# Rope halves exchanged by ScalarE, shared key tiles, and another order of both mixers in a four-layer transformer kernel

## What is computed

```
# mixer A: u, va, q, k, v, qi, ki, wi, g_a, g_b = split(h @ w_in)
y_a = (gelu(u) * spatial(layer_norm(gelu(va)))) @ w_pa    # spatial: a causal 128x128 token mix in each of 4 groups
q, k, qi, ki = rope(...)                     # 8 heads of 64; halves x1, x2: x1*cos - x2*sin, x2*cos + x1*sin
score = sum_h relu(qi_h . ki) * wi_h         # the top 64 keys of each query are kept
y_b = attention(q, k, v, kept keys) @ w_pb
out = (sigmoid(g_a) * y_a + sigmoid(g_b) * y_b) @ w_out
# mixer B: four branches on h = rmsnorm(x), 4 heads of 64
a: window attention at three dilations      b: latent attention, rope on 32 of 96 columns (kpe shared by the heads)
c: compressed blocks (kc, vc -> gelu MLP) + selected keys (ks, vs) + window keys (kw, vw), gated
d: stick-breaking attention
merged = sum_i sigmoid(h @ w_merge_i + b_i) * ((y_i * silu(gate_i)) @ w_branch_i);   x = x + merged @ w_out
```

## Time and profile before

| | us |
|---|---|
| median of 3 runs | 1652.29 (1651.14 to 1652.61) |
| the profiled execution | 1651.31 |
| its span | 1649.5 |
| PE busy | 1594.4 (97%) |
| DVE, ACT, POOL busy | 504.5, 366.6, 1000.3 |
| mean granted clock of PE | 0.976 |

### The profile page before, as it was taken

One profiled execution on the slowest core, in us unless ns is written; L12 is line 12 of the kernel. 1 busy time (PEld: TensorE's weight loads), 2 busy tenths in 40 slices (PEclk: granted clock), 3 DMA queues, 4 the chain that ended last, 5 costly groups with the idle time before them and its releaser, 6 DMA issues.

```text
span 1649.5 us, 32224 instructions
## 1 busy us (share of the span) xinstructions
PE 1594.4 (97%) x14172; PEld 1396.0 (85%) x14172; DVE 504.5 (31%) x1128; ACT 366.6 (22%) x902; POOL 1000.3 (61%) x542
## 2 busy tenths in 40 slices
PE   7999999999999999999999999979999999999998
PEld 5888788887888888878888888868788887788887
DVE  3111264343110211125534311133433233533323
ACT  2111124212110211111422211023333122324212
POOL 6777555666777577764566677744165664346571
PEclk9999999999999999999999999979989999989999
DMA  9565444554555465544455555534354554434461
GB/s 358 202 205 205 141 173 160 179 205 163 200 203 203 176 214 201 201 167 154 162 176 201 178 201 198 197 104 158 132 175 144 198 179 164 150 127 167 173 205 52
DMA packets 42619, 294.90 MB, mean 179 GB/s; under 512 B 4720, under 2 KB 6256, under 8 KB 7792
## 3 DMA queue, kind: packets, MB, share of 16 engines
q1 hardware_dynamic: 42480, 292.84, 50.9%
HBM read 291.78 MB, written 1.05 MB: 178 GB/s over the span
## 4 chain that ended last, share of the span: by engine, by line
PE 95%; DVE 2%; ACT 1%; issue 1%; POOL 0%; DMA 0%; SPq 0%; DVEq 0%; ACTq 0%
PE ps L510 27%; PE ps L511 27%; PE ps L512 27%; PE ps L528 2%; PE ps L530 1%; PE ps L529 1%; PE ps L760 1%; PE ps L596 1%; PE ps L602 1%; PE ps L614 1%; PE ps L588 1%; PE ps L586 0%; DVE diag L1199 0%; POOL w_low L486 0%; DMA ring<-in_w 0%
## 5 line engine op out<-in xcount | busy, mean ns | idle before, releaser
L486 POOL TENSOR_TENSOR w_low<-ring 128x1024 f16<-128x1024 f32 (+2 forms) x538 | 1000.1, 1883 | 616.6 <-DMA ring<-in_w 616.5
L510 PE MATMUL ps<-hP,ring 128*128 128x256 f16 (+1 forms) x2976 | 820.5, 276 | 14.1 <-DVE hP L1209 11.7
L511 PE MATMUL ps<-hP,ring 128*128 128x256 f16 (+1 forms) x2976 | 819.9, 276 | 0.0
L512 PE MATMUL ps<-hP,w_low 128*128 128x256 f16 (+1 forms) x2976 | 819.3, 275 | 0.0
L510 PEld LDWEIGHTS ps<-hP,ring 128*128 128x128 bf16 (+1 forms) x2976 | 294.7, 99 | 62.3 <-DVE hP L1209 13.8
L511 PEld LDWEIGHTS ps<-hP,ring 128*128 128x128 bf16 (+1 forms) x2976 | 294.7, 99 | 36.9
L512 PEld LDWEIGHTS ps<-hP,w_low 128*128 128x128 f16 (+1 forms) x2976 | 294.9, 99 | 36.6
L511 PE MATMUL ps<-work,ring 128*128 128x256 f16 x1088 | 296.7, 273 | 0.0
L510 PE MATMUL ps<-work,ring 128*128 128x256 f16 x1088 | 296.5, 272 | 0.0
L512 PE MATMUL ps<-work,w_low 128*128 128x256 f16 x1088 | 296.3, 272 | 0.0
L1242 DVE TENSOR_TENSOR ps<-work,ps 128x256 f32<-128x256 f32 x88 | 37.8, 429 | 342.1 <-PE ps L512 312.0
(11 more groups left out here) (199 smaller groups left out, 1142.2 us busy)
## 6 DMA issues: line engine op xcount, KB each, us to landing
...
```

The source lines that it names most:

```text
L486: nc.gpsimd.tensor_tensor(w_low[:, c % SLOTS, a:b], ring[:, c % SLOTS, a:b], w_high[:, c % SLOTS, a:b], ALU.subtract).then_inc(split.by((c ...
L510: nc.tensor.matmul(bank, w_high[:, slot, a:a + m], rhs(k, 0), start=(k == 0), stop=False)
L511: nc.tensor.matmul(bank, w_high[:, slot, a:a + m], rhs(k, 1), start=False, stop=False)
L512: mm = nc.tensor.matmul(bank, w_low[:, slot, a:a + m], rhs(k, 0), start=False, stop=(k == kt - 1))
```

## The change

Four things change.
1. The exchange of rope halves leaves TensorE. ScalarE copies 32 partitions at a time crosswise from the bank's first half to its second (`swap`, four copies a tile in A, two in B and one more for each bq to bring its unrotated rows to SBUF). `rotate` on VectorE does the cosine product, the sine product and the addition in one go after it. So that the two halves lie 32 partitions apart in B, the rope columns of kpe and bq are padded with zeros: these tiles have 128 rows instead of 96. SBUF copies (`raw`) and the exchange matrices are gone.
2. ks and kw share one product tile (kc), and so do kc and vc (cmp): two tiles fewer in each mixer B. ScalarE takes kc in four copies of 64 partitions, VectorE takes cmp in eight additions.
3. In A, u and va are made before ga; the layer norm's statistics run before `normalise(s, 1)`, the root follows the copy of turn 1, `y_parts(1)` stands between the two halves of the norm, and the token mix comes after ga5.
4. In B, almost every tile changes its place: qc, kc and cvg before turn(a), the latent branch's products after scores(s), turn(s) between the two hid tiles. Merges 0 to 4 of branch 0 stand around turn(b); the later ones fill the steps of the compressed and stick-breaking branches up to merge (2, 1). `PAIR_B` gives their banks.

The diff, cut to its core (inside functions the indentation is cut by 16):

```diff
-TILES_A = [(kind, n) for kind, m in (("qi", 4), ("ki", 1), ("wi", 2), ("q", 4), ("k", 4), ("v", 4), ("ga", 8), ("u", 4),
-                                     ("va", 4), ("gb", 8)) for n in range(m)]
-TILES_B = [("aq", 0), ("aq", 1), ("ak", 0), ("ak", 1), ("cq", 0), ("ckv", 0), ("rk", 0), ("av", 0), ("av", 1), ("lat", 0),
-           ("ag", 0), ("ag", 1), ("qc", 0), ("rkv", 0), ("qc", 1), ("bk", 0), ("bk", 1), ("bk", 2), ("bk", 3), ("bv", 0),
-           ("bv", 1), ("bq", 0), ("bq", 1), ("kc", 0), ("bq", 2), ("bq", 3), ("kc", 1), ("cvg", 0), ("cvg", 1), ("cmp", 0),
-           ("cmp", 1), ("cg", 0), ("cg", 1), ("bg", 0), ("bg", 1), ("hid", 0), ("hid", 1), ("dq", 0), ("dq", 1), ("kcmp", 0),
-           ("vcmp", 0), ("dk", 0), ("dk", 1), ("dv", 0), ("dv", 1), ("dg", 0), ("dg", 1)]
+TILES_A = [(kind, n) for kind, m in (("qi", 4), ("ki", 1), ("wi", 2), ("q", 4), ("k", 4), ("v", 4), ("u", 4),
+                                     ("va", 4), ("ga", 8), ("gb", 8)) for n in range(m)]
+TILES_B = [("aq", 0), ("aq", 1), ("ak", 0), ("ak", 1), ("cq", 0), ("ckv", 0), ("rk", 0), ("av", 0), ("lat", 0), ("av", 1),
+           ("qc", 0), ("qc", 1), ("kc", 0), ("cvg", 0), ("cvg", 1), ("rkv", 0), ("ag", 0), ("ag", 1), ("cmp", 0), ("cg", 0),
+           ("cg", 1), ("bk", 0), ("bk", 1), ("bk", 2), ("bk", 3), ("bv", 0), ("bv", 1), ("bq", 0), ("bq", 1), ("bq", 2),
+           ("bq", 3), ("hid", 0), ("hid", 1), ("bg", 0), ("bg", 1), ("dq", 0), ("dq", 1), ("dk", 0), ("dk", 1), ("dv", 0),
+           ("dv", 1), ("kcmp", 0), ("vcmp", 0), ("dg", 0), ("dg", 1)]
...
+PAIR_B = {8 * br + n: 2 * ((n + 1) % 2) if br < 3 else 4 + 2 * (n % 2) for br in range(4) for n in range(8)}
...
-def swap(s, t, m, bank, copied, matrix):
-    pe.wait_ge(*raw_copied.at((s,) + t))
-    pe.wait_ge(*cos_done.at((s,) + t))
-    nc.tensor.matmul(ps[0:m, bank, T:2 * T], matrix, copied[0:m, :], start=True, stop=True
...
     first_tiles(s, [(s, "qi", n) for n in range(4)])
     gemm("ki", 0)
-    turn_pairs("qi", 0), turn_pairs("qi", 1)
     gemm("wi", 0), gemm("wi", 1)
-    turn_pairs("qi", 2), turn_pairs("qi", 3)
-    gemm("q", 0)
-    turn_pairs("ki", 0)
-    gemm("q", 1)
-    turn_pairs("q", 0)
+    gemm("q", 0), gemm("q", 1)
     for p, (kind, n) in enumerate((("q", 2), ("q", 3), ("k", 0), ("k", 1))):
         logits(p)
         gemm(kind, n)
-        turn_pairs(*ROPED_A[6 + p])
-    gemm("k", 2)
-    turn_pairs("k", 1)
-    gemm("k", 3)
-    turn_pairs("k", 2)
-    gemm("v", 0)
-    turn_pairs("k", 3)
-    gemm("v", 1), gemm("v", 2)
+    gemm("k", 2), gemm("k", 3)
+    gemm("v", 0), gemm("v", 1), gemm("v", 2)
     pe.wait_ge(*scored.at((s, 7, 1)))
     pe.wait_ge(*taken(s, ("k", 3)))
     unit(0)
-    gemm("v", 3), gemm("ga", 0), gemm("ga", 1), gemm("ga", 2)
+    gemm("v", 3), gemm("u", 0), gemm("u", 1), gemm("u", 2), gemm("u", 3)
     turn(s, 0)
-    gemm("ga", 3)
+    gemm("va", 0)
     values(0)
-    gemm("ga", 4)
+    gemm("va", 1)
     pe.wait_ge(*y_low.at((s, 0)))
     unit(1)
-    gemm("ga", 5), gemm("ga", 6), gemm("ga", 7), gemm("u", 0)
+    gemm("va", 2), gemm("va", 3), gemm("ga", 0), gemm("ga", 1), gemm("ga", 2)
     turn(s, 1)
-    gemm("u", 1)
+    gemm("ga", 3)
     values(1)
-    gemm("u", 2), gemm("u", 3)
-    gemm("va", 0), gemm("va", 1), gemm("va", 2), gemm("va", 3)
-    gemm("gb", 0), gemm("gb", 1), gemm("gb", 2)
...
                                   gmlp("w_s")[:, g * P:g * P + P], start=True, stop=True)
         mm.then_inc(tokens_mixed.by((s, g)), 1)
-    for n in range(5, 8):
+    gemm("ga", 6), gemm("ga", 7)
...
-    gemm("cq", 0), gemm("ckv", 0), gemm("rk", 0), gemm("av", 0)
-    turn_pairs("rk", 0)
-    gemm("av", 1)
+    gemm("cq", 0), gemm("ckv", 0), gemm("rk", 0), gemm("av", 0), gemm("lat", 0), gemm("av", 1)
     pe.wait_ge(*taken(s, ("ak", 1)))
     scores(s, "a", lambda h: head(a_qkT, 0, h), lambda h: head(a_qkT, 2, h))
-    gemm("lat", 0), gemm("ag", 0), gemm("ag", 1), gemm("qc", 0), gemm("rkv", 0), gemm("qc", 1)
+    gemm("qc", 0), gemm("qc", 1), gemm("kc", 0), gemm("cvg", 0), gemm("cvg", 1), gemm("rkv", 0), gemm("ag", 0)
+    turn(s, "a")
+    gemm("ag", 1)
+    mix(s, "a", lambda t, h: a_v[:, t, h * HD:h * HD + HD])
+    gemm("cmp", 0)
+    pe.wait_ge(*y_low.at((s, "a")))
+    pe.wait_ge(*taken(s, ("kc", 0)))
+    scores(s, "s", lambda h: head(c_qkT, 0, h), lambda h: half(c_qkT[:, 2, :], h))
+    gemm("cg", 0), gemm("cg", 1)
     for n in range(4):
         gemm("bk", n)
     gemm("bv", 0), gemm("bv", 1)
-    turn(s, "a")
-    gemm("bq", 0), gemm("bq", 1), gemm("kc", 0)
-    mix(s, "a", lambda t, h: a_v[:, t, h * HD:h * HD + HD])
-    turn_pairs("bq", 0)
-    gemm("bq", 2)
-    turn_pairs("bq", 1)
-    gemm("bq", 3), gemm("kc", 1)
-    turn_pairs("bq", 2), turn_pairs("bq", 3)
-    pe.wait_ge(*y_low.at((s, "a")))
-    pe.wait_ge(*taken(s, ("kc", 1)))
-    scores(s, "s", lambda h: head(c_qkT, 0, h), lambda h: half(c_qkT[:, 2, :], h))
-    gemm("cvg", 0), gemm("cvg", 1), gemm("cmp", 0), gemm("cmp", 1), gemm("cg", 0)
+    for n in range(4):
+        gemm("bq", n)
+    gemm("hid", 0)
     turn(s, "s")
-    gemm("cg", 1)
+    gemm("hid", 1)
     mix(s, "s", lambda t, h: c_vg[:, t, 0:HD])
     gemm("bg", 0)
     pe.wait_ge(*mixed_taken.at((s, "s")))
     scores(s, "w", lambda h: head(c_qkT, 0, h), lambda h: half(c_qkT[:, 3, :], h))
-    gemm("bg", 1), gemm("hid", 0), gemm("hid", 1)
+    gemm("bg", 1), gemm("dq", 0), gemm("dq", 1), gemm("dk", 0), gemm("dk", 1)
     turn(s, "w")
-    gemm("dq", 0)
+    gemm("dv", 0)
     mix(s, "w", lambda t, h: c_vg[:, t, HD:P])
-    gemm("dq", 1)
+    gemm("dv", 1)
     pe.wait_ge(*mixed_taken.at((s, "w")))
     pe.wait_ge(*taken(s, ("bq", 3)))
-    scores(s, "b", lambda h: b_qT[0:96, h, :], lambda h: b_kT[0:96, h, :])
-    gemm("kcmp", 0), gemm("vcmp", 0), gemm("dk", 0), gemm("dk", 1), gemm("dv", 0), gemm("dv", 1)
+    scores(s, "b", lambda h: b_qT[:, h, :], lambda h: b_kT[:, h, :])
+    gemm("kcmp", 0), gemm("vcmp", 0), gemm("dg", 0), gemm("dg", 1)
+    merge(0, 0), merge(0, 1), merge(0, 2)
     turn(s, "b")
-    gemm("dg", 0)
+    merge(0, 3)
     mix(s, "b", lambda t, h: b_v[:, t, h * HD:h * HD + HD])
-    gemm("dg", 1)
-
...
 
-    def copy_raw(kind, n):
-        r = ROPED_A.index((kind, n))
+    def swap(kind, n):
+
+        b = BANK_A[kind, n]
         act.wait_ge(*done.at((s, kind, n)))
-        if r >= 4:
-            act.wait_ge(*swapped.at((s,) + ROPED_A[r - 4]))
-        nc.scalar.activation(raw[:, r % 4, :], ps[:, BANK_A[kind, n], 0:T], ACT.Copy
-                             ).then_inc(raw_copied.by((s, kind, n)), 1)
+        for q in range(4):
...
-    exps(s, 1)
-    take("ga", 6), take("ga", 7)
-    take("u", 0)
     copy_turned(s, 1)
-    take("u", 1)
-    y_parts(1)
-    take("u", 2), take("u", 3)
-    for n in range(4):
-        take("va", n)
     act.wait_ge(*variance.at(s))
     nc.scalar.activation(small[:, 20:22], small[:, 13:16:2], ACT.Sqrt, bias=eps[:, 0:1]
                          ).then_inc(deviation.by(s), 1)
-    for n in range(5):
-        take("gb", n)
+    take("ga", 3)
+    y_parts(1)
...
+    def swap(kind, n):
+
+        b = BANK_B[kind, n]
         act.wait_ge(*done.at((s, kind, n)))
-        if r >= 2:
-            act.wait_ge(*swapped.at((s,) + ROPED_B[r - 2]))
-        nc.scalar.activation(raw2[0:96, r % 2, :], ps[0:96, BANK_B[kind, n], 0:T], ACT.Copy
-                             ).then_inc(raw_copied.by((s, kind, n)), 1)
+        if kind == "bq":
+            nc.scalar.activation(b_qT[0:HD, n, :], ps[0:HD, b, 0:T], ACT.Copy)
+        nc.scalar.activation(ps[64:96, b, T:2 * T], ps[96:P, b, 0:T], ACT.Copy)
+        nc.scalar.activation(ps[96:P, b, T:2 * T], ps[64:96, b, 0:T], ACT.Copy
...
+        elif kind == "kc":
+            for w in range(2):
+                for o in (0, HD):
+                    ins = nc.scalar.activation(c_qkT[o:o + HD, 2 + w, :], ps[HD * w:HD * w + HD, b, 0:T], ACT.Copy)
...
+    gate("cg", 0)
+    exps(s, "s")
+    gate("cg", 1)
     take("bv", 0), take("bv", 1)
...
+    gate("dg", 0)
     exps(s, "b")
-    take("dk", 1), take("dv", 0), take("dv", 1)
+    gate("dg", 1)
...
-def cosines(s, t, rows, bank, cos, dst):
-    dve.wait_ge(*raw_copied.at((s,) + t))
-    nc.vector.tensor_tensor(dst, ps[rows, bank, 0:T], cos, ALU.mult).then_inc(cos_done.by((s,) + t), 1)
-
-def sines(s, t, rows, bank, sin):
+def rotate(s, t, rows, bank, cos, sin, product):
+
     dve.wait_ge(*swapped.at((s,) + t))
+    nc.vector.tensor_tensor(product, ps[rows, bank, 0:T], cos, ALU.mult).then_inc(cos_done.by((s,) + t), 1)
     nc.vector.tensor_tensor(ps[rows, bank, T:2 * T], ps[rows, bank, T:2 * T], sin, ALU.mult
                             ).then_inc(turned_done.by((s,) + t), 1)
+    dve.wait_ge(*cos_done.at((s,) + t))
     dve.wait_ge(*turned_done.at((s,) + t))
...
+    normalise(s, 1)
...
+            y_parts(1)
     for g in range(4):
         dve.wait_ge(*tokens_mixed.at((s, g)))
...
+    shifts(s, "a", scale, alibi_a)
     normalise(s, "a")
-    gate("ag", 1)
```

(12 more changed lines are left out.)

319 lines of the change are left out of this document (144 added, 175 removed).

## The result

The changed kernel takes **1643.39 us** (median of 14 executions, 1636.93 to 1648.92), the kernel before beside it 1652.45 (14, 1650.93 to 1653.81): a ratio of 0.9943, 95% interval 0.993 to 0.9957. It is faster by 9 us where 21 were forecast, and 1643 lies above the range of 1621 to 1639. The profiled execution took 1644.45, its span 1642.6, with a mean granted clock of 0.970; before it was 0.976.

The account below looks back on a forecast made before the run. TensorE was taken to bound the kernel, busy 1594 of 1649.5 us. Removed 15.8 + 10.5 + 3.7 = 30.0, added 9.2, net −20.8 us: forecast 1631, range 1621 to 1639.

Parts of the forecast that it names:

- Part 1: Rope swaps, A and B: 36 swaps of 0.44 us leave TensorE, 15.8 us; ScalarE copies cost 0.33 us each.
- rival 3: ScalarE's bank-to-bank copies are dear; at 0.8 us a copy the kernel is slower, 1661 us; chance 0.02.
- the slack of 2 us: Mixer A at turn(0): VectorE's work was counted to be ready 2 us before TensorE needs it.
- walk: Hand count of some sixty VectorE operations in mixer A against TensorE's list, called no better than 2 us.
- Part 3: A's new order: the token mix waits 2.1 us for v_normed, 4.2 in two mixers, bounds 0 to 3.5.
- Part 2: Shared kc and cmp tiles in B: two tiles of 2.62 us fewer a mixer, 10.5 us in both.
- Part 5: Clock in B: the low stretch of 10.3 us at the hid products stays, at the same price.
- The closing list: Signs to check; the prediction is wrong if low clock follows a new wait or waits for GpSimd's halves appear.
- Part 4: B's new order: three old waits go, 3.7 us; new waits of 1.7 (bk3) and 0.8 (merge(0,1)) a mixer.
- (b): In B, merge(0,1) waits for gate dg1: 9.9 us against TensorE's 9.1, so 0.8 a mixer, bounds 0 to 2.
- Rival 1: In B, a turn between two hid products keeps the clock up: 2 × 4.7 us less, 1622; chance 0.12.
- Rival 2: VectorE bounds mixer A, late at unit(0), turn(1) or v_normed: 4 to 8 us lost, 1635 to 1639; chance 0.22.

Follow-up runs that it names:

- the second experiment: Kernel before with ScalarE's exchange in mixers A only, plus ga3 moved ahead of turn(0) and u2 ahead of turn(1): 1645.8 us, ratio 0.9949.
- the interleaving: Changed kernel with hid products back after scores(w), their 16 matmuls each spread between steps of dq and dk product tiles: 1626.79 us, ratio 0.9837.

## Why the prediction was wrong

The sign was right and the size was not: 9 us of the 20.8 came, and the time lies 4 us outside the range.

**Part 1, copies and swaps: right.** 351 ns a copy against 0.33 as taken; rival 3 is excluded. That the swaps were worth 5.7 us in each A stage holds too, but only behind enough cover, which the second experiment measured (9.7 of 11.4 us in the two stages). What fell is the slack of **2 us at turn(0)**, which the prediction found by its walk. TensorE waited 0.84 and 0.74 us. The slack was spent by two operations of the kept-key sets, which VectorE reached at another moment. First VectorE of the kernel after, then its GpSimd, then VectorE of the kernel before:

```profile
250.49 1.73 DVE L1314 TENSOR_SCALAR work<-work 128x384 f32<-128x384 f32 x1
252.25 2.13 DVE L1315 TENSOR_TENSOR work<-work,con 128x384 f32<-128x384 f32 x1
```

```profile
250.11 3.86 POOL L481 TENSOR_TENSOR w_low<-ring 128x1024 f16<-128x1024 f32 x2 [1.65 <-DMA ring<-in_w]
```

```profile
253.91 0.36 DVE L1354 TENSOR_SCALAR work<-work 128x384 f32<-128x384 f32 x1
254.30 0.56 DVE L1355 TENSOR_TENSOR work<-work,con 128x384 f32<-128x384 f32 x1
```

The same two operations took 3.9 us inside GpSimd's subtraction (250.11 to 253.97) and 0.9 in a gap of it (252.74 to 254.99 in the kernel before). That is 2.9 us of VectorE's list, which has no gap from there to its shifts; less the wait of 0.84 it leaves 2.1, so with the old durations the slack of 2 us was right. In every traced kernel without the swaps in A these two were slow in both mixers (1.27 to 1.73 and 2.13 us); in before, in shared tiles alone and in A's new order with the swaps kept they were short. The Trainium skill ("SBUF — State Buffer", Who interferes with whom), cited in Part 3 for v_normed, bore on this place as well: it says that besides operations with two SBUF inputs also tensor_scalar can take the port that GpSimd shares. The traces agree, with 1.73 against 0.36 us for the one and 2.13 against 0.56 for the other. The walk had taken every duration from the old phase, though the edit takes 5.7 us out of TensorE's list ahead of it.

**Part 2, shared tiles.** 2.62 us a tile is right as TensorE's work. Alone they give half. In the changed kernel the new order hides their waits, but the clock takes its share (Part 5).

**Part 3, v_normed: right as a place, partly lucky in size, wrong in price.** 4.2 us were forecast and 4.5 measured, with 1.17 in one mixer and 3.37 in the other, inside the stated 0 to 3.5. The three other traces with this place unchanged have 6.0 to 6.3 us, so the 4.5 are luck in part. The lengths are collisions, as the prediction argued: VectorE's chain, with y_parts in it, took 7.4 us in the first mixer, with one of its four products long (2.27 us instead of 0.69), and 9.6 in the second, with two long; the 2.2 us between the two chains are the 2.2 between the waits. From the first mixer, then from the second:

```profile
295.72 0.69 DVE L1337 TENSOR_TENSOR work<-work,gm 128x512 f32<-128x512 f32 x1
296.45 2.27 DVE L1338 TENSOR_TENSOR work<-work,gm 128x512 f32<-128x512 f32 x1
...
829.55 2.26 DVE L1337 TENSOR_TENSOR work<-work,gm 128x512 f32<-128x512 f32 x1
...
834.62 2.26 DVE L1337 TENSOR_TENSOR work<-work,gm 128x512 f32<-128x512 f32 x1
```

The bound of 3.5 doesn't come out of the rows: the chain of 7.5 us had two of four products long already, and a third would give 2.1 + 1.6 = 3.7. What the sum lacked is that the long wait had a low stretch right after it. The closing list named just this as what would make the forecast wrong; it should have been a term with bounds.

**Part 4, B's waits: right.** bk3 2.9 against 3.4, merge(0,1) 1.4 against 1.6, and the waits removed are gone. (The terms of (b) for TensorE, 0.4 + 5.2 + 3.3, are 8.9 and not 9.1, which makes its wait 1.0 a mixer and not 0.8; the forecast would be 0.4 higher.)

**Part 5, the clock: this is the step that failed.** "I expect the low stretch to stay, at the same price." It grew from 10.2 to 17.1 us in each mixer; half of the 6.8 more is 3.4 us a mixer, 6.8 in both, more than half of the 11.7 that are missing. The argument was made on the turn alone, and it called the turn's matmuls as short as hid's, where the rows have 128 columns against 15. In the kernel before, hid and the turn behind it (turn(w)) were followed by a product tile, and the clock came back there. The changed order puts the latent branch's short products ahead of the hid tiles, the turn between them and mix(s) behind. What should have been asked is not whether the turn restores the clock, but what full tiles are left on either side of hid and of the turn. Which of the three neighbours did it, no run separates; that the hid products in a row are needed for it, the interleaving shows (17.1 to 0). Part 5 cites the Trainium skill ("TensorE: Matmul & The Clock Gate", Part 4) on transposes; that the low level lasts through the turn agrees with it (2.80 us, turn(w) in the kernel before and turn(s) in the one after), but between product tiles a turn ran at the full level (1.47 us). Rival 1 stood on the same place with the sign turned. Its price of 4.7 us for a stretch of 10.2 was not measured by itself: in the second mixer B, interleaving took a stretch of that length away and 5.7 us with it, a part of which is the cheaper matmuls.

**The bill.** Forecast −20.8. Add 6.8 (low clock in B), 1.7 (low clock behind the wait in the second A), 1.7 (3.4 us more of low clock at the start of the SwiGLU behind it), 1.8 (turn(0) and unit(0)), and take off 0.4 for the other waits: −9.2. The medians are 9.1 apart, but these terms come from the profiled executions, whose spans are 6.9 apart, so 2.3 us stay open, 0.2 to 0.8 in each of several stages. What sets the stretch in the SwiGLU is open too. It doesn't hang on the v_normed wait: it is 3.4 us long in the kernel with the exchange alone and 6.8 in that without a v_normed wait; and behind the first mixer A one execution of the changed kernel has 3.4 and the other 6.8. Rival 2 had 4 to 8 us lost in A, and of the 7.2 that the A stages should have given 4.9 are missing. VectorE late at unit(0), turn(0) and v_normed made 2.1 of them, the low clock 1.7, and 1.1 are open. Its size came true, and only in part by its mechanism.
